# The last group of experts and the final norm: scatter by pairs of experts on row halves, another order of work, one root

## The reference

```python
# x: (1, 256, 1024); 32 experts with a hidden width of 256, two of them for each token
h2 = rms_norm(x, norm_ffn_gain)
hg = einsum('td,edf->tef', h2, w_gate)
hu = einsum('td,edf->tef', h2, w_up)
act = silu(hg) * hu * combine[..., None]       # combine is zero but for a token's two experts
x = x + einsum('tef,efd->td', act, w_down)
y = rms_norm(x, norm_final_gain)               # mean of squares over 1024, root, gain
```

## Time and profile before

| what | value |
|---|---|
| time, median of 3 runs | 469.94 us (469.45 to 470.28) |
| the profiled execution: its own time | 470.17 us |
| the profiled execution: span | 468.4 us, mean granted clock 0.971 |
| TensorE busy | 437.4 us, 93% |
| VectorE, ScalarE, GpSimd busy | 202.0, 122.8 and 12.5 us |
| read from HBM | 134.59 MB |

### The profile page before, as it was taken

The page is one execution under the profiler, slowest core; times in us unless marked ns, Lnnn a source line. Parts: engine busy times, 40 slices in busy tenths (PEclk is TensorE's granted clock), DMA queues, the critical chain, the costliest instruction groups (busy, mean ns, idle before and its releaser), DMA issues.

```text
span 468.4 us, 10279 instructions
## 1 busy us (share of the span) xinstructions
PE 437.4 (93%) x4337; PEld 328.4 (70%) x4337; DVE 202.0 (43%) x568; ACT 122.8 (26%) x313; POOL 12.5 (3%) x37
## 2 busy tenths in 40 slices
PE   9999999999999999999999999999997977797683
PEld 8885688874888888888645777768684745665351
DVE  1376367996343551613200654344463123413224
ACT  5002522001132312220012733324242212312134
POOL 6010100000000000000000000000000000000001
PEclk9999999999999999999999999999999787989898
DMA  8969957706504042255598989999999999999982
GB/s 310 407 212 332 411 193 254 278 26 211 183 11 171 23 157 62 118 180 181 195 421 372 348 333 422 418 417 420 419 420 419 422 418 418 421 420 421 415 332 99
DMA packets 38193, 136.87 MB, mean 292 GB/s; under 512 B 9600, under 2 KB 9920, under 8 KB 26240
## 3 DMA queue, kind: packets, MB, share of 16 engines
q1 hardware_dynamic: 33776, 135.22, 73.1%
q10 hardware_dynamic: 4368, 0.95, 1.1%
HBM read 134.59 MB, written 1.57 MB: 291 GB/s over the span
## 4 chain that ended last, share of the span: by engine, by line
PE 65%; DMA 20%; DVE 9%; SPq 3%; issue 2%; ACT 1%; POOLq 0%; ACTq 0%; DVEq 0%
PE ps L890 23%; DMA arena<-in_moe_w_up 12%; PE ps L1268 8%; PE ps L1131 6%; PE ps L1146 6%; DMA ring<-in_moe_w_up 6%; PE ps L1321 3%; PE ps L1311 3%; PE ps L1226 2%; DVE arena L1645 2%; DVE arena L1642 2%; SPq L398 2%; DMA arena<-in_w_in 2%; PE ps L917 2%; PE ps L1276 1%
## 5 line engine op out<-in xcount | busy, mean ns | idle before, releaser
L890 PE MATMUL ps<-arena 128*128 128x256 f32 (+1 forms) x640 | 157.0, 403 | 0.4 <-DMA arena<-in_w_in 0.4
L890 PEld LDWEIGHTS ps<-arena 128*128 128x128 f32 x640 | 119.8, 190 | 29.9 <-issue 14.9
L1268 PE MATMUL ps<-arena 128*32 128x128 f32 x1072 | 41.9, 299 | 13.1 <-DMA arena<-in_moe_w_up 12.9
L1268 PEld LDWEIGHTS ps<-arena 128*32 128x32 f32 x1072 | 32.5, 117 | 20.5 <-DMA arena<-in_moe_w_up 15.3
L1268 PE MATMUL ps<-ring,arena 128*32 128x128 f32 x912 | 34.1, 293 | 7.1 <-DMA ring<-in_moe_w_up 7.1
L703 ACT ACTIVATE gains<-ps 32x256 f32<-32x256 f32 x62 | 23.3, 376 | 56.2 <-PE ps L1311 55.8
L1268 PEld LDWEIGHTS ps<-ring,arena 128*32 128x32 f32 x912 | 26.8, 114 | 12.2 <-DMA ring<-in_moe_w_up 8.1
L1947 DVE TENSOR_TENSOR masks<-ps,masks 128x64 f32<-128x64 f32 x32 | 7.2, 225 | 59.9 <-ACT masks L684 59.7
L1963 DVE COPY arena<-ps 32x256 f32<-32x256 f32 x62 | 25.8, 416 | 11.2 <-PE ps L1311 10.3
L1146 PE MATMUL ps<-arena 128*128 128x512 f32 x64 | 28.3, 595 | 0.0
L1226 PE MATMUL ps<-masks,arena 128*128 128x128 f32 x224 | 28.3, 287 | 0.0
(11 more groups left out here) (286 smaller groups left out, 453.6 us busy)
## 6 DMA issues: line engine op xcount, KB each, us to landing
arena<-in_w_in SPq DMA_DIRECT2D x9, 2048.0 KB, 7.9
arena<-in_moe_w_gate SPq DMA_DIRECT2D x16, 1024.0 KB, 24.0
arena<-in_moe_w_up SPq DMA_DIRECT2D x16, 1024.0 KB, 25.2
arena<-in_moe_w_down SPq DMA_DIRECT2D x16, 1024.0 KB, 23.9
ring<-in_moe_w_down SPq DMA_DIRECT2D x15, 1024.0 KB, 26.6
ring<-in_moe_w_gate SPq DMA_DIRECT2D x14, 1024.0 KB, 23.3
ring<-in_moe_w_up SPq DMA_DIRECT2D x14, 1024.0 KB, 24.8
arena<-in_w_out SPq DMA_DIRECT2D x2, 2048.0 KB, 7.8
```

The lines of the kernel that those rows point to most:

```text
L890: last = pe.matmul(out, lhs, rhs, start=(k == 0 and (i > 0 or part % 2 == 0)), stop=(k == KD - 1), skip_group_check=(i == 0))
L1268: last = pe.matmul(c.ps[ROWS * q:ROWS * (q + 1), i % 2, 0:P], c.Hg[:, k, ROWS * i:ROWS * (i + 1)], w[:, :, start:start + 127:2], start=(k ...
```

## The change

Only the path with `nwin == 1` (no expert has more than 32 tokens), its last group, and the final norm are changed. `closing` takes the place of `rolling(..., final=True)` on TensorE, ScalarE and VectorE.

- Order on TensorE: `turn_act` of 28, `scatter` of group 6 and the four transposes `turn_pairs` stand before `hidden` of 29 with its wait. `hidden` of 31 is split: six early blocks before `hidden` of 30, the last two after `down` of 29.
- Pairs: `down_pair` puts quarter q of expert i on partitions 32 (2 (q mod 2) + i mod 2) of bank 2 or 3. One copy `take_half` of 128x256 by VectorE then holds two experts and one half of the columns: the even quarter on rows 0 to 63, the odd one on 64 to 127. `scatter_pair` multiplies the halves of rows separately, four matmuls with 64 rows and 256 columns for each pair and half, in steps in which the two row halves write different banks, and waits for its own matmuls after each step. VectorE doubles the selection matrix for it (`ohw_pair`, `S_pair`).
- Pair 0 is scattered between `hidden` and `turn_act` of 31; for pair 1 the left half is scattered in two parts, around the right half of `down` of 31.
- On ScalarE `sigmoid` of 31 and the load of the root's table stand before `copy_turned` of 30.
- Final norm: one root for both tiles, after all four pieces are squared. The left piece of tile 1 is copied and squared by VectorE, the other three by ScalarE. ScalarE scales both left halves; GpSimd does nothing. Tile 1 is written in two halves, the left one from ScalarE's queue.

```diff
+        def down_pair(i, at, halves):
...
+            for half in halves:
+                if i >= 2:
+                    pe.wait_ge(s["z_ready"], half + 1)
+                for kk in range(2):
+                    for q in (2 * half, 2 * half + 1):
+                        at_ = ROWS * (2 * (q % 2) + i % 2)
+                        last = pe.matmul(c.ps[at_:at_ + ROWS, 2 + half, 0:256], c.actT[i % 2][:, kk * ROWS:(kk + 1) * ROWS],
+                                         c.down_w[slot][:, kk, 256 * q:256 * (q + 1)], start=(kk == 0), stop=(kk == 1))
             last.then_inc(s["down_ready"], 1)
...
+        def scatter_pair(pair, halves, step, ends=False):
+
+            for half in halves:
+                pe.wait_ge(s["z_ready"], 2 * pair + half + 1)
+                for tile in range(2):
+                    t = (tile + step) % NT
+                    rows = slice(64 * tile, 64 * tile + 64)
+                    done = pe.matmul(y_out(c, half, t)[:, 256 * tile:256 * tile + 256], c.S_pair[rows, TOK * pair + P * t:TOK * pair + P * t + P],
+                                     c.zt[2 * pair + half][rows, :], start=False, stop=False, skip_group_check=True)
+                    done.then_inc(s["rows_apart"], 1)
+                    apart[0] += 1
+            pe.wait_ge(s["rows_apart"], apart[0])
+            if ends:
+                pe.sem_inc(s["last_scatter"], NT)
...
+        def closing(grp, at):
+
+            unit, had = grp * GROUP, sum(EARLY)
+            turn_act(unit, 0)
+            scatter(grp - 1)
+            turn_pairs(grp)
+            hidden(grp, 1, at[1], True, False)
+            pe.wait_ge(s["Se_ready"], grp + 1)
+            down_pair(0, at[0], (0, 1))
+            turn_act(unit + 1, 1)
+
+            pe.wait_ge(s["early_loaded"], 64)
+            hidden(grp, 3, at[3], False, False, range(had))
+            hidden(grp, 2, at[2], True, False)
+            down_pair(1, at[1], (0, 1))
+            turn_act(unit + 2, 2)
+            pe.wait_ge(s[f"gateup{at[3][0]}"], at[3][1] * 32)
+            hidden(grp, 3, at[3], False, False, range(had, KD))
+            for step in range(2):
+                scatter_pair(0, (0, 1), step)
+            turn_act(unit + 3, 3)
+            down_pair(2, at[2], (0, 1))
+            down_pair(3, at[3], (0,))
+            scatter_pair(1, (0,), 0)
+            down_pair(3, at[3], (1,))
+            scatter_pair(1, (0,), 1, True)
+            for step in range(2):
+                scatter_pair(1, (1,), step, step == 1)
...
+        def take_half(pair, half, ready):
+
+            v.wait_ge(s["down_ready"], ready)
+            v.tensor_copy(c.zt[2 * pair + half], c.ps[:, 2 + half, 0:256]).then_inc(s["z_ready"], 1)
...
+            gate(unit + 1, 1, True, False)
+            gate(unit + 2, 2, True, False)
+            take_half(0, 0, unit + 2)
+            take_half(0, 1, unit + 2)
+            gate(unit + 3, 3, True, False)
+            take_half(1, 0, unit + 4)
+            take_half(1, 1, unit + 5)
...
+            copy_turned(unit + 1, 1, False)
+            sigmoid(unit + 2, 2, False)
+            sigmoid(unit + 3, 3, False)
+            act.activation(c.scratch, c.eps, ACT.Sqrt)
+            copy_turned(unit + 2, 2, False)
+            copy_turned(unit + 3, 3, False)
...
+    act.wait_ge(s["ss2_ready"], 1)
+    act.activation(c.rx, c.ssx, ACT.Sqrt, scale=1.0 / D, bias=c.eps).then_inc(s["r2_root"], 1)
+    act.wait_ge(s["r2_ready"], 1)
+    act.wait_ge(s["y_ready"], 2)
+    for t in range(NT):
+        act.activation(c.y[:, t, 0:512], c.y[:, t, 0:512], ACT.Copy, scale=c.rx[:, t:t + 1]).then_inc(s["out_left_ready"], 1)
+    act.wait_ge(s["out_left_ready"], NT)
+    act.dma_start(io["out"].rearrange("b (t p) d -> p (b t) d", p=P)[:, 1, 0:512], c.y[:, 1, 0:512]).then_inc(s["out_stored"], 16)
...
+    v.wait_ge(s["last_scatter"], 2)
+    left1 = c.end_squares[:, 512:1024]
+    v.tensor_copy(left1, y_out(c, 0, 1)).then_inc(s["left_copied"], 1)
+    v.wait_ge(s["left_copied"], 1)
+    v.scalar_tensor_tensor(out=c.extra[:, 1024:1536], in0=left1, scalar=1.0, in1=left1, op0=ALU.mult, op1=ALU.mult,
+                           accum_out=c.ss_piece[:, 1:2]).then_inc(s["left_squared"], 1)
     v.wait_ge(s["gfin_loaded"], 16)
+    v.tensor_tensor(c.y[:, 1, 0:512], left1, c.gfin[:, 0:512], ALU.mult).then_inc(s["y_ready"], 1)
+    v.wait_ge(s["squares_done"], 1)
+    v.tensor_tensor(c.y[:, 0, 0:512], y_out(c, 0, 0), c.gfin[:, 0:512], ALU.mult).then_inc(s["y_ready"], 1)
+    v.wait_ge(s["left_squared"], 1)
+    v.wait_ge(s["squares_done"], 3)
+    v.tensor_tensor(c.ssx, c.ss_piece[:, 0:2], c.ss_piece[:, 2:4], ALU.add).then_inc(s["ss2_ready"], 1)
+    v.wait_ge(s["r2_root"], 1)
+    v.reciprocal(c.rx, c.rx).then_inc(s["r2_ready"], 1)
+    v.wait_ge(s["r2_ready"], 1)
     for t in range(NT):
...
         v.scalar_tensor_tensor(out=c.y[:, t, 512:D], in0=y_out(c, 1, t), scalar=col(c.rx, t), in1=c.gfin[:, 512:D],
                                op0=ALU.mult, op1=ALU.mult).then_inc(s["out_right_ready"], 1)
```

More of the change, by code:

```diff
@@ L134, in lay_out @@
     c.extra = sb("extra", [P, 4096])
+    c.S_pair = c.extra[:, 0:512]
+    c.ohw_pair = c.extra[:, 512:1024]
     c.gu_w = [r[:, 0:4096].rearrange("p (g k f) -> p g k f", g=2, k=KD) for r in c.ring + [c.extra]]
@@ L1276, in turn_act @@
             pe.transpose(c.ps[:, i % 2, 0:P], c.act[i % 2], c.ident).then_inc(s["act_turned"], 1)
-        def down_half(i, at, half):
+        def down_pair(i, at, halves):
             slot, times = at[2:4]
-            pe.wait_ge(s["last_down" if half else f"down{slot}"], 16 if half else times * 16)
-            if half == 0:
-                pe.wait_ge(s["actT_ready"], EXPERTS)
-                pe.wait_ge(s["out_copied"], 2 * EXPERTS - 4)
-            for kk in range(2):
-                for q in (2 * half, 2 * half + 1):
-                    last = pe.matmul(down_out(c, i, q), c.actT[i % 2][:, kk * ROWS:(kk + 1) * ROWS], c.down_w[slot][:, kk, 256 * q:256 * (q + 1)],
-                                     start=(kk == 0), stop=(kk == 1))
-            last.then_inc(s["down_ready"], 1)
@@ L1291, in scatter_last @@
-        def scatter_last(grp):
-            pe.wait_ge(s["out_copied"], 2 * EXPERTS - 2)
-            for t in range(NT):
-                for half in range(2):
-                    pe.wait_ge(s["stacked_right" if half else "stacked_left"], 2)
-                    pe.matmul(y_out(c, half, t), c.S_e[:, t * P:(t + 1) * P], c.Y[half],
-                              start=False, stop=False, skip_group_check=True).then_inc(s["last_scatter"], 1)
+            if 0 in halves:
+                pe.wait_ge(s[f"down{slot}"], times * 16)
+                pe.wait_ge(s["actT_ready"], EXPERTS - GROUP + i + 1)
+            else:
+                pe.wait_ge(s["last_down"], 16)
@@ L1323, in scatter, with rolling @@
             last.then_inc(s["scattered"], 1)
-        def rolling(grp, at, following, first, final):
+        def rolling(grp, at, following, first):
             for i in range(GROUP):
                 unit = grp * GROUP + i
-                if final and i == GROUP - 2:
-                    turn_act(unit, i)
-                    hidden(grp, i + 1, at[i + 1], True, first)
-                    turn_act(unit + 1, i + 1)
-                    down(unit, i, at[i], True, first)
-                    for half in range(2):
-                        down_half(i + 1, at[i + 1], half)
-                    pe.wait_ge(s["Se_ready"], grp + 1)
-                    scatter_last(grp)
-                    break
                 after = (grp, i + 1, at[i + 1]) if i < GROUP - 1 else (grp + 1, 0, following)
-                more = not final or i < GROUP - 1
-                if more:
-                    hidden(*after, True, first, range(KD // 2))
+                hidden(*after, True, first, range(KD // 2))
                 turn_act(unit, i)
-                if more:
-                    hidden(*after, True, first, range(KD // 2, KD))
+                hidden(*after, True, first, range(KD // 2, KD))
                 if i == 0 and not first:
@@ L1351, in rolling @@
                     pe.wait_ge(s["Se_ready"], grp + 1)
-                if i == 2 and not final:
+                if i == 2:
                     gather(grp + 1, unit * 2 - 2)
```

126 lines of the change are left out of this document (54 added, 72 removed).

## The result

| | kernel before | changed kernel |
|---|---|---|
| time, median of 6 runs each on one chip | 469.87 us (469.45 to 470.28) | 473.43 us (472.73 to 474.56) |
| ratio, 95% interval | | 1.0072 [1.0062, 1.0083] |
| profiled execution: own time, span | 470.17, 468.4 us | 474.56, 472.8 us |
| granted clock, mean | 0.971 | 0.963 |
| end of the last scatter, E | 461.97 | 463.31 |

The forecast was 471.4 us, and slower as the likeliest sign. The sign holds; the loss is 3.56 us instead of 1.5, and the time lies above the upper end of the range, 472.8.

A forecast was written before the change was run, and what follows sets the result against it. The second half was taken to wait for expert weights, so only work behind the last landings counted: -0.25 (E) + 1.73 (norm) + 0 (output) = +1.5 us, so 471.4 us; likeliest case 470.9 to 472.1, 8 in 10 within 469.6 to 472.8.

The forecast's parts named there:

- The sign: Whole kernel: slower, +0.3%, chance 0.67; within 0.2% 0.21, faster 0.12.
- The early part: Group 6's moved scatter up to `hidden` of 30, ending at 449.9: costs nothing, 0.15 us of slack before 447.75.
- From the landing to E: From down of 29's weights landing (450.03) to the last scatter's end: E at 461.65 to 461.75, before 461.97.
- The two steps of pair 0: Scatter of pair 0 on TensorE: row halves run together, 1.2 us a step, from 452.65 to 455.0.
- the rule of the Trainium skill: Rival: left half of 31 runs behind `down` of 30, not beside it; E 0.9 us later, 472.3; chance 0.1.
- The base: Kernel before: E at 461.97, second output transfer issued at 464.16, E + 2.19.
- gain 0.25 us on E: End of the last scatter: all the pairs buy is about 0.25 us against 461.97.
- the term of +1.73: Final norm, E to last issue: second square +0.74, VectorE's sum +0.24, second product +0.75; E + 3.9 instead of E + 2.19.
- a bound of 0 to +0.3: VectorE's left-piece work, 3.1 us from about 460.2, ends just with the squares; no slack, may bind by this much.
- The output: Last issue to the end of the span: change counted as 0, bounds -0.4 (two queues) and +0.3 (smaller packets).
- The sum: Whole change: -0.25 at E, +1.73 in the norm, 0 for the output, +1.5 us.
- the one of the clock: Rival: clock falls in the loosely packed part, 3.4 us at half rate costing 1.7 less 0.3 slack; 472.8; chance 0.06.

The follow-up runs named there:

- c1: Second profiled execution of the changed kernel, nothing altered; ratio to the kernel before 1.0073.
- e5: Kernel before with only the scatter of group 6 and its turned weights moved ahead of the wait for expert 29; ratio 1.0002.
- e10: Changed kernel with VectorE's and ScalarE's norm inside the conditional block and tile 1 stored whole from SyncE; ratio to the kernel before 1.0069.
- e1: Changed kernel with VectorE's final norm written inside the conditional block instead of behind it; ratio to the kernel before 1.0071.
- e6: Changed kernel with the final norm of both VectorE and ScalarE inside the conditional block; ratio to the kernel before 1.0078.
- e7: Changed kernel with the norm of the kernel before (a root for each tile), VectorE's part inside the block; ratio to the kernel before 1.0064.
- e11: Changed kernel with VectorE's last two copies and ScalarE's three squares behind the block, so both leave it early; ratio to the kernel before 1.0070.
- e13: Changed kernel with the conditional turned round, so the path taken falls through to the norm without a jump; ratio to the kernel before 1.0174.
- c2: Second profiled execution of the unchanged kernel before; 470.04 us.
- e3: Changed kernel with `down_pair` on four strips instead of two (output not the reference's, same instruction count); ratio to the kernel before 1.0053.
- e12: Kernel before with the conditional turned round, so the path taken falls through to the norm without a jump; ratio 1.0161.
- e2: Kernel before with the new final norm alone and the last scatter ordered left, left, right, right; ratio 1.0036.
- e14: Changed kernel with both engines leaving the block early and the right half of `down` of 31 before pair 1's first scatter step; ratio to the kernel before 1.0050.
- e8: Changed kernel with two roots, VectorE's part in the block, right half of `down` of 31 before pair 1's first scatter step; ratio to the kernel before 1.0069.
- e15: Changed kernel, block left early, right half of `down` of 31 first, TensorE waiting behind the block for the output's landing; ratio to the kernel before 1.0062.
- e9: Kernel before with the new final norm alone, both engines' part of it inside the conditional block; ratio 1.0027.

## Why the prediction failed, step by step

**The early part** held. `hidden` of 30 ends at 450.0 in c1 (449.9 forecast), and the moved scatter costs and gives nothing (e5).

**From the landing to E.** 11.6 us forecast, 12.14 or 12.15 in six of the seven later executions with this order on TensorE (12.26 in e10; c1, e1, e6, e7, e11 and e13 the others). By pieces, in c1, with the landing at 450.35:

```profile
453.09 2.36 PE L1301 MATMUL ps<-arena,extra 64*128 64x256 f32 x16
...
456.71 0.41 PE L1281 MATMUL ps<-arena,masks 128*32 128x256 f32 x2
456.91 0.39 PE L1281 MATMUL ps<-ring,masks 128*32 128x256 f32 x2
...
459.15 1.06 PE L1281 MATMUL ps<-arena,masks 128*32 128x256 f32 x8
460.13 0.70 PE L1301 MATMUL ps<-gains,extra 64*128 64x256 f32 x4
...
461.02 1.47 PE L1301 MATMUL ps<-gains,extra 64*128 64x256 f32 x8 [0.18 <-PE ps L1301]
```

The two steps of pair 0 take 2.36 us (2.35 forecast; the pace is a little better and the wait for itself longer than I had them), so the row halves do run together. The left half of 31 runs in turn with `down` of 30 from 456.71 on, on the other two strips, and the right half takes 1.06 (1.05). By the rule of the Trainium skill that matmuls start and end strictly in program order (TensorE: Matmul & The Clock Gate, Part 3: Packing small matmuls) it would have come behind; the trace disagrees here as it did in the earlier trace rows. What I missed is the second step on the left half: it is in front of the right half's steps and waits for itself, so that these start at 461.02 where the copy alone would have let them at 460.75. With `down_pair(2)` 0.2 later than summed, this makes the 0.5.

**The base** was wrong too. E at landing + 11.90 in the profile before holds the half clock behind 440; c2, without it, has 11.15. It cost that kernel nothing, because VectorE's way out covered it. Against 11.15 the change doesn't gain 0.25 us on E, it loses 1.0, of which e3 gives 0.86 to the depth of `down_pair`.

**From E to the issue: the term of +1.73 is the step that failed.** It measured +3.1: E + 5.31 where the sum had E + 3.9. These 1.4 us are the largest part of the 2.1 by which the forecast missed; E gives 0.5. The squares, the sum, the root and the two products are as summed: 3.70 in e6, e11 and e13. But I let VectorE's strand start at the left pieces' release, and named it as a bound of 0 to +0.3. It starts 2.1 us later, behind the way out of the block. e11 and e13 leave the strand's work alone, one leaving the block early, the other without a jump, and both have 3.70. This cause of the late issue is shown. That the time would fall with it is not: in these runs the output took back what the issue gained. The way out was to be seen beforehand: in the trace of before, the first instruction behind the block (L2029 at 460.67) starts 0.6 us after its named releaser is done, and 2.9 us after VectorE's branch.

**The output: 0 forecast, 0 to +0.9 in the changed kernel.** In the table above the landing follows the fetches: 3.06 to 3.44 with none in the stream (e12, e13, e2), 3.75 to 4.7 where 8 KB ones or the end of a 16 KB one lie in it, 4.83 to 5.30 in all seven with a 16 KB one starting after the last issue. The packets fit this: in e6, e11 and e14 the first of the last 16, which run one at a time, starts 3.11 to 3.13 us after the last issue, where the 16 KB fetch ends (3.12 to 3.15), while in e2, e12 and e13 all packets have ended by 3.1. So one share of the output seems to stand still while the engine that serves it fetches. It is why e6 to e8, e10, e11 and e14 don't repay what they gain at the issue. That the fetch is the cause is argued from this order of 20 executions and from the packets, not shown by taking it alone away: e15 failed to, and e12 and e13 changed the entry as well.

**The sum** from the landing to the last issue is 14.1 us in both executions of the kernel before, and 17.45 in c1: +3.35, with 0 to 0.9 for the output, where the medians differ by 3.56. With the ways out gone in both kernels (e13 against e12) the change costs 0.99 at E, 1.53 at the issue and 0.37 behind it, 2.9 us from the landing to the output, in one execution of each. The times show less: the medians are 478.86 and 477.69 us, 1.2 apart, and the intervals of the two ratios overlap, since the landing itself comes 1.16 us earlier in e13's profile. That the change would be slower also without the ways out is likely from the timelines; the times alone don't show it. No rival of the prediction describes this; the one of the clock gave 472.8, and the second execution shows that it isn't needed.

## What to carry to other kernels

Ask of each engine when it leaves a conditional, not only what it waits for: in the trace, compare the start of the first instruction behind the block with the moment at which its named releaser was done. If that gap is open on the last chain, put the leaving into an idle stretch; an engine with no such stretch passes the cost on. And take a "gain" on the last matmul only against what really sets the next instruction: when two executions with different E issue at the same time, E isn't on the path.

## What the runs showed of the hardware

- Leaving the conditional block cost 2.6 to 3.1 us from the branch to the next instruction on VectorE and ScalarE (461.08 to 463.92 in the changed kernel, 460.74 to 463.47 in e2, 461.97 to 464.55 in e1, 457.62 to 460.67 in c2), and 3.2 to 3.9 on TensorE (the length of its branch, 3.87 in the changed kernel and 3.25 in e15). A transfer of 8 KB of kind "instruction" starts about 1.0 us after the branch and takes 0.3 to 0.6; TensorE's are of 16 KB and take 0.9 to 1.5. The branch instruction itself is recorded with 0.04 to 0.05 us on VectorE and ScalarE. The Trainium skill states the mechanism (Runtime: NRT & Kernel Launch, Instruction fetch mechanics): a branch that is taken to a target outside the instructions held makes the engine fetch them by DMA before it goes on. The trace agrees.
- ScalarE's way out took 4.4 to 4.8 us when it lay beside the output's transfers (e6, e9), and the entry into the turned conditional 4.0 to 4.2 us on VectorE and 6.2 to 6.3 on ScalarE (0.5 to 0.6 with the path taken first).
- Matmuls with 64 rows and 256 columns on the two row halves run together, at 0.21 to 0.22 us for a pair. The wait for its own last matmuls costs a step 0.37 us, by the difference of two forms: the four pairs of a step on both halves take 1.23 us to the start of the next step (453.90 to 455.13), the two pairs of the later ones 0.80 to the next work (459.16 to 459.96).
